# Low parts of the activations on VectorE, and two key chunks projected between the turns of the token tiles

## The chip, the cores and the metric

The kernel runs on one core of one Trainium2 chip, with its engines TensorE (PE), VectorE (DVE), ScalarE (ACT), GpSimd (POOL) and SyncE (SP). The metric is device time of one execution in microseconds, as the median of several runs.

## What is computed

One inference step of a one-layer hybrid decoder: 16 meta tokens and 1024 prompt tokens, with 8 single decode tokens beside them, 1048 tokens in all. Cut to the part that matters here:

```python
def rms_norm(x, g):
    xf = x.astype(jnp.float32)
    y = xf * lax.rsqrt(jnp.mean(xf * xf, axis=-1, keepdims=True) + EPS)
    return (y * g.astype(jnp.float32)).astype(x.dtype)
...
    n = rms_norm(x, g_mix)
    q, k, v, xr, gr, gates = jnp.split(n @ w_in, SPLITS, axis=-1)
...
    attn = attend(q, k, v, sb_bias.reshape(N_KV_HEADS, GROUP))
...
    x = x + (gate_a * attn + gate_b * rnn) @ w_out
...
    x = x + (jax.nn.gelu(ua) * ub) @ w_down
```

The first stage of the kernel makes n, turned so that the model dimension lies on the partitions, and from it k, v and q. All later stages (attention and the recurrent branch, output projection, FFN) are the same in both kernels.

## The kernel before

The stages are blocks that all five engines enter and leave together. The change lies in the first one, `phase_qkv`. Its inputs are 9 token tiles (tile 0 has 24 rows, tiles 1 to 8 have 128 each) and 12 weight tiles of 128 output columns: key tiles j = 0, 1, value tiles j = 2, 3, then 8 query tiles.

**Token tiles.** For tile t, in turn: SP loads it (`load_x`); ACT squares it with a running sum (`square`, L279); DVE makes the mean (L337), ACT its root (L292), DVE the reciprocal (L342) and the scaled rows in place (L343); PE turns it in 8 transposes into PSUM `xt` (L419); DVE multiplies by the gain into `tmp` (L356); ACT rounds `tmp` to the high part `n_hi` (L298); POOL takes tmp - n_hi as the low part `n_lo` (L260). `xt` and `tmp` have two halves that tiles use in turn. ACT and DVE run these loops with one tile's lag between the first steps and the last: in turn t, DVE does the mean, reciprocal and scaling of tile t and then the gain of tile t-1.

**Weights.** A weight tile is loaded into one of two slots of `w_raw`; ACT rounds it to `w_hi` (L285), POOL makes `w_lo` (L254).

**Projections.** `project` (L87) makes one chunk of 350 token columns: for each of 8 parts k of the model dimension three matmuls (high by high, weight high by activation low, weight low by activation high), 24 in all, summed in one of two PSUM banks `proj`. ACT takes it out (`evacuate`, L308) into `kv_ch` or `q_stage`. There are 3 chunks per weight tile; chunk 0 needs token tiles 0 to 3, chunk 1 tiles 0 to 6, chunk 2 all. Before the change PE starts them only when `lo_ready` shows all 9 tiles, and goes weight tile by weight tile. A slot's next `w_hi` is made by ACT behind the middle chunk of the following tile. After the four key and value tiles PE turns them back to token rows (L448), DVE copies these (L386) and SP stores them; then come the query tiles in a loop.

**Orders.** Every engine runs its list in the order written; semaphores (`lo_ready`, `w_lo_ready`, `proj_out` and others) tie them together. SP issues all transfers on one queue.

## Time and profile before

| | us |
|---|---|
| median of 3 runs | 2277.09 |
| lowest and highest | 2276.91, 2279.01 |
| the profiled execution | 2274.87 |
| its span in the trace | 2273.1 |

The profiled execution is 1.77 us longer than its span: that lies around the first and last instruction. All durations below are from this one execution. A row of the timeline gives the start, the duration, the engine and line, the instruction with output and inputs, how often it stands in a row, and in brackets how long its engine was idle before and what ended that.

### The profile page before, as it was taken

How to read it: one execution, taken by the hardware profiler on the slowest of the kernel's cores; microseconds unless marked ns; L12 is line 12 of the kernel's file. 1: busy time of each engine (PE TensorE's matmuls, PEld its weight loads, DVE VectorE, ACT ScalarE, POOL GpSimd, SP SyncE). 2: the span in 40 equal slices, each digit the busy share in tenths (PEclk: the TensorE clock that was granted, in tenths of full speed). 3: DMA queues.
4: the chain of work that ended last, by engine and by line, in shares of the span. 5: the costliest groups of instructions: out<-in, count | busy, mean ns of one | idle time of the engine just before them, and what ended most of it. 6: DMA issues, size and time to landing. Idle time of an engine off the chain costs nothing. (4 is left out here: it accounts for less than half of the span.)

```text
span 2273.1 us, 41388 instructions
## 1 busy us (share of the span) xinstructions
PE 1961.5 (86%) x14580; PEld 1773.7 (78%) x14580; DVE 1210.3 (53%) x2020; ACT 938.1 (41%) x1514; POOL 247.6 (11%) x117
## 2 busy tenths in 40 slices
PE   4997988879797978879798597899999999999985
PEld 3897867767685867758586386899999999999985
DVE  6101557556484756647474632655554555545555
ACT  4122567566656647666665411212221222212213
POOL 4121000000000000000000400312221222112210
PEclk9998999989899998989898798999999999999988
DMA  3233313131222212131221222111111111111104
GB/s 120 80 99 98 78 37 92 30 98 36 78 57 74 76 33 78 40 92 51 72 62 50 96 87 70 43 42 46 46 37 37 55 47 46 37 37 46 46 19 165
DMA packets 197465, 144.01 MB, mean 63 GB/s; under 512 B 58037, under 2 KB 186102, under 8 KB 197268
## 3 DMA queue, kind: packets, MB, share of 16 engines
q1 hardware_dynamic: 197294, 141.79, 21.7%
q8 instruction: 99, 1.62, 0.3%
q14 instruction: 72, 0.59, 0.1%
HBM read 124.38 MB, written 17.61 MB: 62 GB/s over the span
## 5 line engine op out<-in xcount | busy, mean ns | idle before, releaser
L87 PE MATMUL d_p_up<-n_hi,d_w_hi 128*128 128x350 f32 x1056 | 343.7, 325 | 14.0 <-POOL d_w_lo L1656 7.7
L87 PE MATMUL d_p_up<-n_lo,d_w_hi 128*128 128x350 f32 x1056 | 342.6, 324 | 0.0
L87 PE MATMUL d_p_up<-n_hi,d_w_lo 128*128 128x350 f32 x1056 | 342.4, 324 | 0.0
L87 PE MATMUL b_p_proj<-n_hi,b_w_hi 128*128 128x350 f32 x768 | 274.0, 357 | 53.6 <-ACT r_gr L990 32.6
L1803 DVE TENSOR_TENSOR mix<-mix,d_p_down 128x350 f32<-128x350 f32 x264 | 137.3, 520 | 325.1 <-PE d_p_down L1850 325.1
L1700 ACT ACTIVATE d_up<-d_p_up 128x350 f32<-128x350 f32 x132 | 60.6, 461 | 502.2 <-PE d_p_up L87 502.2
L87 PE MATMUL b_p_proj<-n_lo,b_w_hi 128*128 128x350 f32 x768 | 257.2, 335 | 0.0
L87 PE MATMUL b_p_proj<-n_hi,b_w_lo 128*128 128x350 f32 x768 | 256.6, 334 | 0.0
L941 ACT ACTIVATE b_sums<-b_p_z,b_bias 128x720 f32<-128x720 f32 (+16 forms) x136 | 94.8, 697 | 304.7 <-PE b_p_z L1222 256.4
L87 PEld LDWEIGHTS d_p_up<-n_hi,d_w_hi 128*128 128x128 f32 x1056 | 200.5, 190 | 15.0 <-POOL d_w_lo L1656 8.1
L87 PEld LDWEIGHTS b_p_proj<-n_hi,b_w_hi 128*128 128x128 f32 x768 | 154.7, 201 | 72.5 <-ACT r_gb L990 29.9
L87 PEld LDWEIGHTS d_p_up<-n_hi,d_w_lo 128*128 128x128 f32 x1056 | 200.5, 190 | 0.0
L87 PEld LDWEIGHTS d_p_up<-n_lo,d_w_hi 128*128 128x128 f32 x1056 | 200.4, 190 | 0.0
L1053 DVE TENSOR_TENSOR_SCAN b_sums<-b_sums 128x720 f32<-128x720 f32 (+16 forms) x136 | 171.1, 1258 | 21.5 <-ACT b_sums L977 16.2
L1850 PE MATMUL d_p_down<-d_a_hi,d_wd_hi 128*128 128x350 f32 x480 | 159.3, 332 | 23.8 <-DVE d_a_lo L1794 23.8
L1039 DVE COPY mix<-b_p_misc 128x64 f32 (+2 forms) x136 | 30.1, 221 | 271.8 <-PE b_p_misc L1253 264.1
L1656 POOL TENSOR_TENSOR d_w_lo<-w_raw,d_w_hi 128x1024 fp32r<-128x1024 f32 x45 | 114.2, 2548 | 519.7 <-ACT d_w_hi L1686 519.7
L1215 PE MATMUL b_p_z<-b_k_in,b_q_in 64*64 64x360 f32 (+16 forms) x1024 | 103.1, 464 | 76.8 <-issue 31.7
L1850 PE MATMUL d_p_down<-d_a_hi,d_wd_lo 128*128 128x350 f32 x480 | 158.2, 330 | 0.0
L1850 PE MATMUL d_p_down<-d_a_lo,d_wd_hi 128*128 128x350 f32 x480 | 157.7, 329 | 0.0
L87 PEld LDWEIGHTS b_p_proj<-n_lo,b_w_hi 128*128 128x128 f32 x768 | 153.5, 200 | 0.0
L87 PEld LDWEIGHTS b_p_proj<-n_hi,b_w_lo 128*128 128x128 f32 x768 | 152.6, 199 | 0.0
(248 smaller groups left out, 3921.7 us busy)
## 6 DMA issues: line engine op xcount, KB each, us to landing
w_raw<-in_w_in SPq DMA_DIRECT2D x45, 512.0 KB, 4.9
w_raw<-in_w_up SPq DMA_DIRECT2D x45, 512.0 KB, 3.9
b_page<-in_cache_k SPq DMA_DIRECT2D x128, 128.0 KB, 2.2
b_page<-in_cache_v SPq DMA_DIRECT2D x128, 128.0 KB, 2.1
w_raw<-in_w_down SPq DMA_DIRECT2D x22, 512.0 KB, 3.2
b_q_in<-q_scr SPq DMA_DIRECT2D x272, 32.0 KB, 2.2
q_scr<-a_q_stage SPq DMA_DIRECT2D x16, 260.0 KB, 3.4
mix<-in_x_prompt SPq DMA_DIRECT2D x8, 512.0 KB, 7.5
```

The lines of the kernel that those rows point to most:

```text
L87: last = pe.matmul(out, w[:, k, :], x[:, k, col:col + CW], start=(k == 0 and w is w_hi and x is x_hi), stop=(k == KT - 1 and w is w_lo))
L941: own.mark(act.activation(so, pz, ACT.Abs, bias=bias[:, 0:1]))
L1039: dve.tensor_copy(g.mix[:, bass.ds(i if s >= 0 else i - 1, 1), FIRST + q0:FIRST + q0 + nq] .rearrange("p a c -> p (a c)"), p_av[:, 0:nq]). ...
L1053: dve.tensor_tensor_scan(pos[:, ::-1], so[:, ::-1], pos[:, ::-1], 0.0, ALU.add, ALU.add)\
L1215: last = pe.matmul(banks[bank][QB * a:QB * (a + 1), 0:k1 - k0], q_in[rows, Q_AT[s], a, :], k_in[rows, k0:k1], start=True, stop=k1 <= diagonal)
L1656: pool.tensor_tensor(w_lo[:, slot, :, :], w_raw[:, raw, :, :], w_hi[:, slot, :, :].bitcast(F32), ALU.subtract).then_inc(lo_ready, 1)
L1700: act.activation(up[:, u % 2, CW * c:CW * (c + 1)], p_up[:, n % 2, 0:CW], ACT.Copy).then_inc(up_out, 1)
L1803: dve.tensor_tensor(to, to, p_down[:, n % 4, 0:CW], ALU.add).then_inc(down_out, 1)
L1850: last = pe.matmul(p_down[:, n % 4, 0:CW], w[:, k, P * tile:P * (tile + 1)], a[:, k, CW * c:CW * (c + 1)], start=(k == 0 and w is wd_hi an ...
```

## The change

1. **Low parts.** POOL's loop over the token tiles is gone. In turn t, DVE makes the low part of tile t-2 behind the gain of tile t-1; the mean of tile t+1 is taken a turn earlier. ACT squares two tiles ahead instead of one, so that the square of tile 1 stands ahead of the first root. Behind its turns 5 and 7 DVE also makes `w_lo` of the first two weight tiles; POOL keeps the other ten. ACT rounds these two weights in its turns 5 and 7 (before: 7 and 9).
2. **Order of chunks.** The first six chunks are those of both key tiles in pairs, `FIRST_PIECES` = (0,0), (1,0), (0,1), (1,1), (0,2), (1,2) as (tile j, chunk c). PE does the first half (12 matmuls) of piece 0 behind the transposes of token tile 5 and the second behind those of tile 6, and piece 1 likewise behind tiles 7 and 8; pieces 2 to 5 follow. From value tile j = 2 on the order is the old one. ACT takes piece 0 out behind its last `n_hi` and piece 1 just behind that.
3. **Transfers.** The first weight tile is loaded ahead of token tile 4 (before: behind it), the second ahead of tile 6 (before: behind tile 8). Each key tile's store waits for its last piece.

```diff
@@ -87,6 +87,9 @@
             last = pe.matmul(out, w[:, k, :], x[:, k, col:col + CW],
                              start=(k == 0 and w is w_hi and x is x_hi), stop=(k == KT - 1 and w is w_lo))
     return last
+
+
+FIRST_PIECES = [(j, c) for c in range(CHUNKS) for j in range(2)] + [(j, c) for j in (2, 3) for c in range(CHUNKS)]
 
 
 def phase_qkv(nc, g, sem):
@@ -171,9 +174,8 @@
                     sp.dma_start(rows[r:r + n, :], src).then_inc(rows_in, 16)
                 for t in range(2, TILES):
                     load_x(t)
-                    if t == 4:
-                        load_w(0, 1, K_COL)
-                load_w(1, 2, K_COL + P)
+                    if t in (3, 5):
+                        load_w(t // 2 - 1, t // 2, K_COL + P * (t // 2 - 1))
                 sp.dma_start(g.bias_all[:, :], g.sb_bias[0, :].partition_broadcast(P)).then_inc(bias_in, 16)
                 sp.dma_start(g.table[:, :],
                              g.page_table.rearrange("(o a) b -> o (a b)", o=1)).then_inc(bias_in, 16)
@@ -183,7 +185,7 @@
                 for n in (2, 3):
                     load_w(n % 2, n + 1, K_COL + P * n)
                 for j in range(2):
-                    sp.wait_ge(proj_out, 2 + CHUNKS * (j + 1))
+                    sp.wait_ge(proj_out, 2 + FIRST_PIECES.index((j, CHUNKS - 1)) + 1)
                     for h in range(2):
                         sp.dma_start(g.k_scr[2 * j + h, :, :],
                                      kv_ch[HD * h:HD * (h + 1), j, FIRST:LAST]).then_inc(k_stored, 16)
@@ -254,14 +256,6 @@
                     pool.tensor_tensor(w_lo[:, slot, :, :], w_raw[:, slot, :, :],
                                        w_hi[:, slot, :, :].bitcast(F32), ALU.subtract).then_inc(w_lo_ready, 1)
 
-                for t in range(TILES):
-                    c0, nr = token_tile(t)
-                    pool.wait_ge(hi_ready, t + 1)
-                    pool.tensor_tensor(g.n_lo[:, :, c0:c0 + nr], tmp[:, t % 2, :, 0:nr],
-                                       g.n_hi[:, :, c0:c0 + nr].bitcast(F32), ALU.subtract).then_inc(lo_ready, 1)
-                    if t == TILES - 2:
-                        low_part(0, 1)
-                low_part(1, 2)
                 with pool.Fori(0, 5, 1) as i:
                     for s in range(2):
                         low_part(s, nth(i, 2, s + 2))
@@ -284,35 +278,42 @@
                     act.wait_ge(proj_done, chunks)
                     act.activation(w_hi[:, slot, :, :], w_raw[:, slot, :, :], ACT.Copy).then_inc(w_hi_ready, 1)
 
+                def evacuate(bank, index, out, scale):
+                    act.wait_ge(proj_done, index + 6)
+                    act.activation(out, proj[:, bank, 0:CW], ACT.Copy, scale=scale).then_inc(proj_out, 1)
+
+                def kv_piece(p):
+                    j, c = FIRST_PIECES[p]
+                    evacuate(p % 2, p + 1, kv_ch[:, j, CW * c:CW * (c + 1)], 1.0)
+
                 square(0)
+                square(1)
                 for t in range(TILES + 1):
                     if t < TILES:
                         _, nr = token_tile(t)
                         act.wait_ge(meaned, t + 1)
                         act.activation(stat[0:nr, 2, t:t + 1], stat[0:nr, 1, t:t + 1], ACT.Sqrt).then_inc(rooted, 1)
-                    if t + 1 < TILES:
-                        square(t + 1)
+                    if t + 2 < TILES:
+                        square(t + 2)
                     if t:
                         c0, nr = token_tile(t - 1)
                         act.wait_ge(scaled, t)
                         act.activation(g.n_hi[:, :, c0:c0 + nr], tmp[:, (t - 1) % 2, :, 0:nr],
                                        ACT.Copy).then_inc(hi_ready, 1)
-                    if t in (7, 9):
-                        high_part((t - 7) // 2, 3 * (t - 5) // 2, 16)
+                    if t in (5, 7):
+                        high_part((t - 5) // 2, 3 * (t - 3) // 2, 16)
+                    if t == TILES:
+                        kv_piece(0)
                 act.activation(lam[:, 0, :], g.par[:, :, R_LAM], ACT.Abs).then_inc(act_step, 1)
+                kv_piece(1)
                 act.wait_ge(act_step, 1)
                 act.activation(lam[:, 1, :], lam[:, 0, :], ACT.Exp, scale=-1.0).then_inc(lam_exp, 1)
-
-                def evacuate(bank, index, out, scale):
-                    act.wait_ge(proj_done, index + 6)
-                    act.activation(out, proj[:, bank, 0:CW], ACT.Copy, scale=scale).then_inc(proj_out, 1)
-
-                for j in range(4):
-                    for c in range(CHUNKS):
-                        n = CHUNKS * j + c
-                        evacuate(n % 2, n + 1, kv_ch[:, j, CW * c:CW * (c + 1)], 1.0)
-                        if c == 1 and j:
-                            high_part((j + 1) % 2, 3 * (j + 2), 16 * ((j + 1) // 2 + 1))
+                for p in range(2, len(FIRST_PIECES)):
+                    kv_piece(p)
+                    if p in (4, 5):
+                        high_part(p - 4, 6 + p + 1, 32)
+                    if FIRST_PIECES[p] == (3, 1):
+                        high_part(0, 15, 48)
 
                 def q_pair(i, last):
                     for s in range(2):
@@ -330,12 +331,17 @@
             @block.vector
             def _(dve):
                 own = Chain(dve, dve_step)
-                for t in range(TILES + 1):
-                    if t < TILES:
-                        _, nr = token_tile(t)
-                        dve.wait_ge(squared, t + 1)
-                        dve.tensor_scalar(stat[0:nr, 1, t:t + 1], stat[0:nr, 0, t:t + 1], 1.0 / D, EPS,
-                                          ALU.mult, ALU.add).then_inc(meaned, 1)
+
+                def mean(t):
+                    _, nr = token_tile(t)
+                    dve.wait_ge(squared, t + 1)
+                    dve.tensor_scalar(stat[0:nr, 1, t:t + 1], stat[0:nr, 0, t:t + 1], 1.0 / D, EPS,
+                                      ALU.mult, ALU.add).then_inc(meaned, 1)
+
+                mean(0)
+                for t in range(TILES + 2):
+                    if t + 1 < TILES:
+                        mean(t + 1)
                     if t < TILES:
                         _, nr = token_tile(t)
                         dve.wait_ge(rooted, t + 1)
@@ -347,7 +353,7 @@
                         dve.tensor_copy(g.par[:, :, :].rearrange("p k r -> p (k r)"),
                                         pt[:, 0:KT * N_ROWS]).then_inc(params, 1)
                         dve.wait_ge(params, 1)
-                    if t:
+                    if 1 <= t <= TILES:
                         u = t - 1
                         c0, nr = token_tile(u)
                         dve.wait_ge(x_turned, u + 1)
@@ -356,6 +362,17 @@
                         dve.tensor_tensor(tmp[:, u % 2, :, 0:nr], xt[:, u % 2, :, 0:nr],
                                           g.par[:, :, R_GMIX:R_GMIX + 1].to_broadcast([P, KT, nr]),
                                           ALU.mult).then_inc(scaled, 1)
+                    if t >= 2:
+                        u = t - 2
+                        c0, nr = token_tile(u)
+                        dve.wait_ge(hi_ready, u + 1)
+                        dve.tensor_tensor(g.n_lo[:, :, c0:c0 + nr], tmp[:, u % 2, :, 0:nr],
+                                          g.n_hi[:, :, c0:c0 + nr].bitcast(F32), ALU.subtract).then_inc(lo_ready, 1)
+                    if t in (5, 7):
+                        n = (t - 5) // 2
+                        dve.wait_ge(w_hi_ready, n + 1)
+                        dve.tensor_tensor(w_lo[:, n, :, :], w_raw[:, n, :, :], w_hi[:, n, :, :].bitcast(F32),
+                                          ALU.subtract).then_inc(w_lo_ready, 1)
                 dve.wait_ge(bias_in, 32)
                 for h in range(2):
                     dve.tensor_copy(g.bias_pair[HD * h:HD * (h + 1), :], g.bias_all[HD * h:HD * (h + 1), h:HEADS:2])
@@ -410,6 +427,20 @@
             def _(pe):
                 pe.sem_inc(proj_done, 6)
                 pe.wait_ge(consts, 3)
+
+                def first_piece(p, k0, k1):
+                    j, c = FIRST_PIECES[p]
+                    if k0 == 0:
+                        pe.wait_ge(lo_ready, tiles_for_chunk(c))
+                        if c == CHUNKS - 1:
+                            pe.wait_ge(consts, 9)
+                        pe.wait_ge(w_lo_ready, j + 3)
+                        pe.wait_ge(proj_out, p + 1)
+                    last = project_part(pe, proj[:, p % 2, 0:CW], w_hi[:, j % 2], w_lo[:, j % 2],
+                                        g.n_hi, g.n_lo, CW * c, k0, k1)
+                    if k1 == KT:
+                        last.then_inc(proj_done, 1)
+
                 for t in range(TILES):
                     _, nr = token_tile(t)
                     pe.wait_ge(normed, t + 1)
@@ -425,8 +456,12 @@
                             last = pe.transpose(pt[:, N_ROWS * k:N_ROWS * (k + 1)], rows[:, P * k:P * (k + 1)],
                                                 g.ident[0:N_ROWS, 0:N_ROWS])
                         last.then_inc(rows_t, 1)
-                pe.wait_ge(lo_ready, TILES)
-                pe.wait_ge(consts, 9)
+                    if t in (5, 7):
+                        first_piece(t // 2 - 2, 0, KT // 2)
+                    if t in (6, 8):
+                        first_piece(t // 2 - 3, KT // 2, KT)
+                for p in range(2, 6):
+                    first_piece(p, 0, KT)
 
                 def tile(slot, index, first_chunk, base):
                     pe.wait_ge(w_lo_ready, index + 2)
@@ -437,7 +472,7 @@
                                        g.n_hi, g.n_lo, CW * c)
                         last.then_inc(proj_done, 1)
 
-                for n in range(4):
+                for n in (2, 3):
                     tile(n % 2, n + 1, CHUNKS * n, 0)
                 pe.wait_ge(proj_out, 2 + 12)
                 for t in range(TILES):
```

On VectorE, inside the token tiles of the first stage, before the change (a_stat holds the means and roots, mix the token rows, a_xt the turned tile in PSUM, a_tmp the tile times the gain):

```order
L337 TENSOR_SCALAR a_stat<-a_stat 128x1 [waits a_squared]
L342 RECIPROCAL a_stat<-a_stat 128x1 [waits a_rooted]
L343 TENSOR_SCALAR mix<-mix,a_stat 128x1024 [waits a_dve_step]
L356 TENSOR_TENSOR a_tmp<-a_xt,par 128x1024 [waits a_lo_ready,a_x_turned]
L337 TENSOR_SCALAR a_stat<-a_stat 128x1 [waits a_squared]
```

The same engine after the change, turn 5 and the start of turn 6:

```order
L348 RECIPROCAL a_stat<-a_stat 128x1 [waits a_rooted]
L349 TENSOR_SCALAR mix<-mix,a_stat 128x1024 [waits a_dve_step]
L362 TENSOR_TENSOR a_tmp<-a_xt,par 128x1024 [waits a_lo_ready,a_x_turned]
L369 TENSOR_TENSOR n_lo<-a_tmp,n_hi 128x8x128 [waits a_hi_ready]
L374 TENSOR_TENSOR a_w_lo<-w_raw,a_w_hi 128x1024 [waits a_w_hi_ready]
L338 TENSOR_SCALAR a_stat<-a_stat 128x1 [waits a_squared]
```

Each turn has one more operation over a whole tile, and turns 5 and 7 have two more.

On TensorE, the last token tile and the first projection before the change:

```order
L419 MATMUL a_xt<-ident,mix 128x128 [waits a_scaled,a_normed]
L419 MATMUL a_xt<-ident,mix 128x128 x7
L87 MATMUL a_proj<-n_hi,a_w_hi 128x350 [waits a_w_lo_ready,a_proj_out,a_consts,a_lo_ready]
L87 MATMUL a_proj<-n_lo,a_w_hi 128x350
L87 MATMUL a_proj<-n_hi,a_w_lo 128x350
```

After the change, the transposes of tile 5 and the first three of the 12 matmuls behind them:

```order
L450 MATMUL a_xt<-ident,mix 128x128 [waits a_scaled,a_normed]
L450 MATMUL a_xt<-ident,mix 128x128 x7
L87 MATMUL a_proj<-n_hi,a_w_hi 128x350 [waits a_proj_out,a_w_lo_ready,a_lo_ready]
L87 MATMUL a_proj<-n_lo,a_w_hi 128x350
L87 MATMUL a_proj<-n_hi,a_w_lo 128x350
```

The first projection has moved from behind tile 8 to behind tile 5, and the transposes of tiles 6 to 8 stand behind pieces of it.

On ScalarE, the start of the stage before the change:

```order
L279 ACT_TABLE_LOAD
L279 ACTIVATE a_junk,a_stat<-mix 24x1024 [waits a_x_in0]
L292 ACT_TABLE_LOAD
L292 ACTIVATE a_stat<-a_stat 24x1 [waits a_meaned]
L279 ACTIVATE a_junk,a_stat<-mix 128x1024 [waits a_x_in1]
```

And after it:

```order
L273 ACT_TABLE_LOAD
L273 ACTIVATE a_junk,a_stat<-mix 24x1024 [waits a_x_in0]
L273 ACTIVATE a_junk,a_stat<-mix 128x1024 [waits a_x_in1]
L295 ACT_TABLE_LOAD
L295 ACTIVATE a_stat<-a_stat 24x1 [waits a_meaned]
```

The square of tile 1, with its wait for that tile's transfer, now stands ahead of the table load and of the first root.

## Rows read from the trace of the kernel before

**Rows 1.** The page's first part: busy time, share of the span, instructions.

```profile
PE 1961.5 (86%) x14580; PEld 1773.7 (78%) x14580; DVE 1210.3 (53%) x2020; ACT 938.1 (41%) x1514; POOL 247.6 (11%) x117
```

**Rows 2.** Stretches: from:to, length, busy by engine, granted clock, DMA share, GB/s.

```profile
0.00:52.00 52.00, 18.80 (x84) 15.50 (x85) 35.10 (x42) 25.50 (x43) 23.26 (x25) 1.00 0.35 121
56.00:77.00 21.00, 20.88 (x131) 20.59 (x130) 0.22 (x2) 3.73 (x7) 2.39 (x1) 1.00 0.12 31
206.00:213.00 7.00, 0.00 (x0) 0.00 (x0) 1.14 (x7) 1.60 (x5) 1.56 (x6) 0.73 0.33 81
600.00:1200.00 600.00, 505.15 (x4764) 424.98 (x4764) 372.39 (x629) 382.39 (x632) 0.00 (x0) 0.91 0.25 64
```

**Rows 3.** Timeline of VectorE: tile 1's scaling, then a whole turn.

```profile
7.78 0.75 DVE L343 TENSOR_SCALAR mix<-mix,a_stat 128x1024 f32<-128x1024 f32 x1
...
21.74 1.21 DVE L356 TENSOR_TENSOR a_tmp<-a_xt,par 128x1024 f32<-128x1024 f32 x1
...
24.16 0.16 DVE L342 RECIPROCAL a_stat<-a_stat 128x1 f32<-128x1 f32 x1 [1.16 <-ACT a_stat L292]
24.36 2.49 DVE L343 TENSOR_SCALAR mix<-mix,a_stat 128x1024 f32<-128x1024 f32 x1
26.77 1.21 DVE L356 TENSOR_TENSOR a_tmp<-a_xt,par 128x1024 f32<-128x1024 f32 x1
27.90 0.14 DVE L337 TENSOR_SCALAR a_stat<-a_stat 128x1 f32<-128x1 f32 x1
```

**Rows 4.** Timeline of GpSimd in the same turn.

```profile
24.12 2.18 POOL L260 TENSOR_TENSOR n_lo<-a_tmp,n_hi 128x1024 fp32r<-128x1024 f32 x1 [2.85 <-ACT n_hi L298]
```

**Rows 5.** Timeline of ScalarE in the same turn.

```profile
22.98 1.06 ACT L298 ACTIVATE n_hi<-a_tmp 128x1024 fp32r<-128x1024 f32 x1 [2.84 <-DVE a_tmp L356]
23.95 0.18 ACT L292 ACTIVATE a_stat<-a_stat 128x1 f32<-128x1 f32 x1
24.04 1.04 ACT L279 ACTIVATE a_junk<-mix 128x1024 f32<-128x1024 f32 x1
```

**Rows 6.** Timeline of TensorE: tile 4, the first chunk's start and end of its ramp.

```profile
21.87 1.97 PE L419 MATMUL a_xt<-ident,mix 128*128 128x128 f32 x8 [3.06 <-DVE mix L343]
...
50.91 0.66 PE L87 MATMUL a_proj<-n_hi,a_w_hi 128*128 128x350 f32 x1 [6.94 <-POOL n_lo L260]
...
51.66 0.49 PE L87 MATMUL a_proj<-n_hi,a_w_lo 128*128 128x350 f32 x1
51.95 0.50 PE L87 MATMUL a_proj<-n_hi,a_w_hi 128*128 128x350 f32 x1
...
56.04 0.32 PE L87 MATMUL a_proj<-n_hi,a_w_hi 128*128 128x350 f32 x1
56.20 0.32 PE L87 MATMUL a_proj<-n_lo,a_w_hi 128*128 128x350 f32 x1
```

**Rows 7.** Timeline of ScalarE at the start: the second table load.

```profile
4.59 1.28 ACT L292 ACT_TABLE_LOAD   x1
```

**Rows 8.** Transfers issued in stretches of 5.0:5.4, 5.8:6.4 and 6.4:6.8, us to landing.

```profile
mix<-in_x_prompt SPq DMA_DIRECT2D x1, 512.0 KB, 3.8
mix<-in_x_prompt SPq DMA_DIRECT2D x2, 512.0 KB, 5.6
w_raw<-in_w_in SPq DMA_DIRECT2D x1, 512.0 KB, 7.7
```

**Rows 9.** Line 1019, a later stage: VectorE makes a weight's low part (ns min/median/max).

```profile
L1019 DVE TENSOR_TENSOR b_w_lo<-w_raw,b_w_hi x33: 1215/1224/1227, 213.5 to 1215.8; 128x1024 fp32r<-128x1024 f32 x33
```

**Rows 10.** Timelines of GpSimd and TensorE where the third weight tile begins.

```profile
74.12 2.39 POOL L254 TENSOR_TENSOR a_w_lo<-w_raw,a_w_hi 128x1024 fp32r<-128x1024 f32 x1 [20.93 <-ACT a_w_hi L285]
...
76.57 0.43 PE L87 MATMUL a_proj<-n_hi,a_w_hi 128*128 128x350 f32 x1
```

**Rows 11.** Timeline of TensorE: last key and value transposes, first query matmuls.

```profile
109.24 0.66 PE L448 MATMUL a_xt<-ident,a_kv_ch 128*128 128x128 f32 x4 [0.79 <-DVE a_kv_tok L386]
...
109.90 0.33 PE L87 MATMUL a_proj<-n_lo,a_w_hi 128*128 128x350 f32 x1
```

## The prediction

> **What bounds the kernel now.** The page's first part says PE is busy 86% of the span [rows 1], but that is a mean over stages. The stretches show what matters: in the first 52 us PE works 18.8 us, while from 56 to 77 us it is busy 20.88 of 21 [rows 2]. So the first stage has two parts: token tiles, bound by something else, and projections, bound by PE. In the first part the step from one tile to the next is 26.77 - 21.74 = 5.03 us [rows 3]. In that step VectorE's scaling of the rows takes 2.49 us, though the same instruction took 0.75 us on tile 1 [rows 3]. Beside the slow one GpSimd runs its low part from 24.12 to 26.30; the scaling begins at 24.36 and ends at 26.85, which is 0.55 after GpSimd is done [rows 3, 4]. I read this as the scaling waiting for GpSimd. ScalarE's own work per tile is about 2.2 us [rows 5] and the transposes are 1.97 [rows 6], so neither is the bound. PE then waits 6.94 us for the last low parts and starts projecting at 50.91 [rows 6]. The first six chunks last until 76.57, where the third weight tile begins [rows 6, 10]: 25.66 us. Matmuls come 0.29 apart at first (350 columns in 0.29 us is the 1.2 GHz level) and 0.16 apart from 55.7 on [rows 6]. The granted clock of the stretch says 1.00 there [rows 2]; I go by the pace, since the column seems blind until its first change. At full pace a chunk is 24 x 0.161 = 3.86 us, six are 23.2, so the ramp and small waits cost 25.66 - 23.2 = 2.5.
>
> **The tile step after the change.** VectorE alone: reciprocal to scaling 0.20, scaling 0.75 less 0.09 overlap (24.36 + 2.49 = 26.85 against the next start at 26.77) 0.66, gain 1.13 (26.77 to 27.90) [rows 3], new low part 1.14 (1.224 for a like 128x1024 subtraction [rows 9], less the same overlap), mean 0.07: 3.20 us. Its loop with ScalarE: gain 1.21, hand-over 0.04, n_hi 0.97 until the root starts, root 0.18, hand-over 0.04, then 0.20 and 0.66: 3.30 us [rows 3, 5]. The longer one decides, so a tile takes 3.3 us instead of 5.03. The low part's bounds are 1.05 and 1.3; both stay under or near the loop and move the end by 0.2 at most.
>
> **The start gets later.** The square of tile 1 now stands ahead of the table load of 1.28 us that was done by 5.9 [rows 7]. Tile 1's transfer lands near 5.5 (an estimate between the end of the load and 3.8 us after issue as for tile 2 [rows 8]); square with read-out 1.2, load 1.28, so the first root is at 8.0, against 5.9, and tile 0 is turned at 9.2. Running on by the same durations, tile 1 is turned at 11.3 and tile 2 at 13.7.
>
> **The transfers.** Tile 2 landed at 5.1 + 3.8 = 8.9, the first weight tile at 6.4 + 7.7 = 14.1, with tiles 3 and 4 between [rows 8], so about 1.7 us each. The weight now takes tile 4's place and tile 4 lands at about 14.1. ScalarE wants it at 12.5, behind the root of tile 2. It waits 1.6 us, n_hi of tile 1 is queued behind it and VectorE's low part and next root behind that: tile 3 is turned at 17.5. If tile 4 lands at 12.6 the end gains 0.5, if it lands at 15.6 the end loses 1.5. Later tiles land before they are wanted, by the same spacing. Then by 3.3: tile 4 at 20.8 (before: 21.87 [rows 6]), tile 5 at 24.1 (before: one step more, 26.9).
>
> **The pieces.** Behind tile 5 PE waits: n_hi of tile 4 from 25.2, rounding of the weight 26.2 to 27.2, its low part on VectorE 27.3 to 28.5. First half of piece 0 from 28.5: 12 x 0.293 = 3.5 us at the low pace, to 32.05. Transposes of tile 6 to 33.75 (here they delay the gain of tile 6: VectorE now waits for PE). Second half: PE has by then worked without a gap for over 5 us, and in the kernel before the pace rose 4.5 to 5 us into unbroken work [rows 6], so 12 x 0.161 = 1.9, to 35.7. Transposes of tile 7 at the full pace 1.3 (four take 0.66 [rows 11]), to 37.0. Piece 1 waits for the second weight: gain of tile 6 at 34.1, n_hi 35.3, rounding 36.3, low part 37.4 to 38.6. Half 38.6 to 40.6, tile 8 to 41.9, half to 43.8. Piece 2 needs the bank of piece 0, which ScalarE empties only behind the last n_hi: gain of tile 8 at 41.9, n_hi 43.1 to 44.1, out at 44.55. Here a wait of 0.8 us takes the place of the old one. So piece 2 starts at 44.6, four chunks of 3.86 take it to 60.05, and the third weight tile waits 0.2 us for its low part as before: in both orders the rounding stands behind the fifth chunk, and a copy-out of some 0.4 (an estimate: 350 of the 1024 columns that take 1.06 [rows 5]), the rounding of 1.05 [rows 5] and 2.39 on GpSimd [rows 10], with three hand-overs, just outlast the sixth chunk. It begins at 60.3 instead of 76.57.
>
> **Sum.** 76.57 - 60.3 = 16.3 us. Split another way: PE's main run begins 50.91 - 44.6 = 6.3 earlier, with two chunks (7.7) already done, and without the ramp and its small waits (2.3 of the 2.5). Behind the third weight tile nothing in the order has moved, and PE is the bound to the end of the stage, so this arrives at the end. The two key stores and the loads of the next weights come earlier than needed. The constants and bias copies on VectorE (small operations) lie beside the four chunks; if that cover were gone they would cost some 10 us, but PE does not wait for them before the value tiles are turned, 30 us later. In the profiled execution: span 2273.1 - 16.3 = 2256.8, with 1.8 around it 2258.6. The median lay 2.2 above the profiled execution, so 2260.8, **about 2261**.
>
> **One rule against the trace.** PE's clock must hold through the pieces. The trace shows that transposes alone, four per 1.45 us, with idle between, kept it high: the first query matmuls behind them run at the full pace (0.33 at 109.90) [rows 11], while in 7 us without work it fell to a mean of 0.73 [rows 2]. The Trainium skill, TensorE: Matmul & The Clock Gate, section Part 4: PE-mode transpose, says that transposes do not count as busy TensorE in the same way as matmuls. Taken strictly that would leave piece 0 and 1 at the low pace, which is rival B. The trace disagrees as to holding the clock; whether transposes help it to rise is shown nowhere.
>
> **Rivals.**
> B. *The clock stays low through both pieces.* The tile phase of the kernel before never left the low pace, with PE busy 1.97 of 5.03. Then the second half of piece 0 ends at 37.3, tile 7 at 39.0, piece 1 goes 39.0 to 42.5 and 44.2 to 47.7 with tile 8 between. PE never pauses, so piece 2 starts at 47.7. The four chunks pay the ramp once: 25.66 - 7.72 = 17.9, to 65.6. Saved 10.9: **2266.2**. For it: the gaps and the mixed work; against: no pause from 28.5 on.
> C. *The scaling is slow for another reason than GpSimd* (the change does not remove what it means to). With 2.49 kept, VectorE's step is 0.20 + 2.40 + 1.13 + 1.14 + 0.07 = 4.94 and the loop 5.04; tile 5 is turned at 32.8, the second weight and piece 1 come at 49.4, piece 2 at 57.0, the third weight tile at 72.7. Saved 3.9: **2273.2**, no change that counts. Against it: 0.75 whenever GpSimd is idle, and an end 0.55 behind GpSimd's.
> D. *More waits in the tile part than I count*: tile 4 at 16 or later and each turn of the loop 0.5 longer cost 2 + 6 x 0.5 = 5 us: about **2266 to 2270**.
> E. *Slower, by the clock of the later stages.* From 600 to 1200 us the granted clock is 0.91 [rows 2], so about 18% of the time is at the low level (0.5), and when it falls depends on how PE's pauses lie. The whole program moves 16 us, and the pauses may fall otherwise. Over the some 2000 us behind the first stage, with PE bound, a mean lower by 0.01 costs some 20 us. From a mean lower by 0.008 it eats the 16.3; lower by 0.011 it gives **2283**. Against it: the three runs lie within 2.1 us of each other.
>
> **How the numbers follow.** Chances: forecast A (2257 to 2264) 0.66, B 0.16, D 0.08, C 0.05, E 0.05. Predicted is A, 2261. The range: down, the clock already high in the first half of piece 0 (12 x 0.13 = 1.6 less) and tile 4 in time (0.5 less), with 2.4 for the median's own spread, gives 2256.5; up, B with half of the late tile (0.7) and 1.5 of spread gives 2268.5. It leaves out C, E and part of D, and holds some 0.85. A measurement of this kernel can tell about 0.2%, 4.6 us, from no change. Faster by more than that are A, B and D and a little of E, 0.91; within it C and little else, 0.05; slower 0.04.
>
> **What would show it.** The scaling at 0.75 us in every turn and a tile step of 3.2 to 3.5 us (C wrong). ScalarE idle before the square of tile 4. PE's first projection matmul near 28.5, 0.29 apart for about 12 of them and 0.16 in the second half of piece 0; in B all 48 are 0.29 apart. VectorE's gain of tile 6 released by PE. PE released by ScalarE's copy-out at about 44.6, and the third weight tile begun at 60.3. The time from there to the end as before, to 1 or 2 us; if it is longer by more, E is at work. I would be wrong if the low part on VectorE took over 1.7 us, or if ScalarE loaded its table more often than three times in the stage.

## The result, and the profile after

The changed kernel takes 2253.7 us (median of 4, 2248.4 to 2256.7) where the kernel before, timed beside it, takes 2277.0: a ratio of 0.9894, 95% interval 0.9874 to 0.9914. It is 23.3 us faster. The prediction was 2261.0 with a range of 2256.5 to 2268.5, so the direction is right and the saving is 7 us larger than forecast, outside the range. The profiled execution took 2253.84, with 1.8 of it outside the span.

The page's first part of the changed kernel (busy time, share, instructions):

```profile
span 2252.0 us, 41403 instructions
PE 1963.5 (87%) x14580; PEld 1776.4 (79%) x14580; DVE 1205.3 (54%) x2031; ACT 937.9 (42%) x1514; POOL 225.1 (10%) x106
```

As [rows 1], TensorE does the same 14580 matmuls in the same busy time. What went is idle time. The stretches that answer to [rows 2]:

```profile
0.00:52.00 52.00, 31.80 (x171) 29.37 (x172) 34.11 (x68) 26.79 (x46) 1.86 (x14) 0.84 0.38 132
56.00:77.00 21.00, 20.89 (x130) 20.60 (x129) 0.00 (x0) 4.64 (x8) 4.80 (x2) 1.00 0.39 102
...
600.00:1200.00 600.00, 517.03 (x4875) 434.41 (x4873) 376.55 (x642) 379.24 (x636) 0.00 (x0) 0.92 0.23 61
```

In the first 52 us TensorE is busy 31.80 instead of 18.80, which is what was meant. But the last row has moved too, and nothing had been changed there: from 600 to 1200 it is busy 517.03 instead of 505.15, with 4875 matmuls in place of 4764. A stage that the diff does not touch runs faster. That row is the first sign of where the other 7 us are.

Next to [rows 3], VectorE's timeline, a whole turn of the changed kernel:

```profile
20.36 1.22 DVE L362 TENSOR_TENSOR a_tmp<-a_xt,par 128x1024 f32<-128x1024 f32 x1
21.50 1.22 DVE L369 TENSOR_TENSOR n_lo<-a_tmp,n_hi 128x1024 fp32r<-128x1024 f32 x1
...
22.99 0.75 DVE L349 TENSOR_SCALAR mix<-mix,a_stat 128x1024 f32<-128x1024 f32 x1
23.66 1.22 DVE L362 TENSOR_TENSOR a_tmp<-a_xt,par 128x1024 f32<-128x1024 f32 x1
```

The scaling takes 0.75 us instead of 2.49, and the step is 23.66 - 20.36 = 3.30 instead of 5.03, though VectorE now makes the low part as well (1.22). TensorE's timeline with the pieces, next to [rows 6, 10]:

```profile
28.28 0.63 PE L87 MATMUL a_proj<-n_hi,a_w_hi 128*128 128x350 f32 x1 [2.50 <-issue]
...
31.91 1.15 PE L450 MATMUL a_xt<-ident,mix 128*128 128x128 f32 x8
...
34.82 1.03 PE L450 MATMUL a_xt<-ident,mix 128*128 128x128 f32 x8
...
37.72 0.40 PE L87 MATMUL a_proj<-n_hi,a_w_hi 128*128 128x350 f32 x1 [1.87 <-issue]
...
40.32 1.91 PE L450 MATMUL a_xt<-ident,mix 128*128 128x128 f32 x8
...
45.08 0.40 PE L87 MATMUL a_proj<-n_hi,a_w_hi 128*128 128x350 f32 x1 [0.80 <-ACT a_kv_ch L283]
...
60.86 0.43 PE L87 MATMUL a_proj<-n_hi,a_w_hi 128*128 128x350 f32 x1
```

Piece 0 begins at 28.28, piece 1 at 37.72, piece 2 at 45.08 behind ScalarE's copy-out, the third weight tile at 60.86 where [rows 10] had 76.57.

To see where the rest arose, the program is cut at marks that both traces have: the first projection matmul, the first score matmul of attention, the last one, and the end. Times in us, one profiled execution each:

| kernel | first projection | attention begins | attention lasts | from there to the end of the span |
|---|---|---|---|---|
| before | 50.9 | 218.9 | 1011.7 | 1042.5 |
| changed | 28.3 | 204.2 | 1002.7 | 1045.1 |

The first stage gave 14.7 us, attention 9.0, and the rest took 2.6 back. The forecast had 16.3, 0 and 0. The last of the three does not repeat: run again (below), both kernels take 1042.3 us from the last score matmul to the end.

### The profile page after: what moved, and what is told of

Its sections match the earlier page's. It is cut to its first block and busy times, and to the rows that moved or that the text cites. A ratio compares the mean times of both kernels' runs of the same rounds, so it can differ in the third digit from the quotient of the medians.

```text
span 2252.0 us, 41403 instructions
## 1 busy us (share of the span) xinstructions
PE 1963.5 (87%) x14580; PEld 1776.4 (79%) x14580; DVE 1205.3 (54%) x2031; ACT 937.9 (42%) x1514; POOL 225.1 (10%) x106
## 5 line engine op out<-in xcount | busy, mean ns | idle before, releaser
L1088 DVE TENSOR_TENSOR_SCAN b_sums<-b_sums 128x720 f32<-128x720 f32 (+16 forms) x136 | 171.1, 1258 | 20.5 <-ACT b_sums L1012 16.2
```

The lines of the kernel that those rows point to most:

```text
L1088: dve.tensor_tensor_scan(pos[:, ::-1], so[:, ::-1], pos[:, ::-1], 0.0, ALU.add, ALU.add)\
```

## Inside attention: the jump back

The attention loop is one loop of seven passes behind a first pass written out, so there are six jumps back. At the head of each pass TensorE stands idle before the first score product. The view of waits, of TensorE from 350 to 1212 before and to 1205 after (waited for: us in total, times, longest):

```profile
PE b_p_z L1215 <- issue: 31.7, 5, 7.4
...
PE b_p_z L1215 <- DMA b_k_in<-k_scr: 7.3, 1, 7.3
```

```profile
PE b_p_z L1250 <- DMA b_k_in<-k_scr: 19.1, 3, 6.7
...
PE b_p_z L1250 <- issue: 10.2, 3, 3.6
```

The first fence is the kernel before, the second the changed one. "issue" means that the engine waited for nothing that the profile shows. The kernel before has five such waits and one put down to a transfer of keys, 39.0 us in six passes. The changed one has three and three, 29.3 us. The difference, 9.7, is the 9.0 by which attention is shorter. Every second pass loads new keys; there the wait fell only from 6.3 to 7.4 us to 6.0 to 6.7, and it is the transfer that ends it now. In the other three it fell from 5.5 to 6.4 us to 3.3 to 3.6.

Something that the view of waits has no name for holds TensorE at the jump, and for a shorter time after the change. The page's list of DMA queues has a candidate, instructions themselves. The kernel before, then the changed one (packets, MB, share):

```profile
q8 instruction: 99, 1.62, 0.3%
```

```profile
q8 instruction: 93, 1.52, 0.3%
```

Six packets of 16384 bytes fewer, one for each jump. The pieces' extra waits make TensorE's program five instructions longer (8651 against 8646, of 64 bytes, counted in the built programs; the two traces too hold 2032 against 2027 records of TensorE ahead of attention, and all five more are waits), so every later instruction stands five places further on. In the kernel before the loop begins 216 instructions behind a multiple of 256, which is one packet, in the changed one 221. The Trainium skill, Runtime: NRT & Kernel Launch, section Instruction fetch mechanics, says that instructions arrive in blocks of 16 KiB, 256 of them, in sequence, and that a taken branch whose target is not among those at hand has to wait for the block to be fetched. The packets of 16384 bytes agree with it. It does not say that the target's place within its block matters; the runs below show that. The traces show one thing more: not every loop is fetched again. At the jumps of the first stage's query loop (298 instructions in the trace) and of the FFN's (908) the queue has no packet, and the next matmul comes 0.04 to 0.05 us behind the jump, in both kernels. Only the attention loop, with over 2180, brings packets in each pass. Where between 908 and 2180 the limit lies no run here shows.

## Experiments

Each is timed against the kernel before, run beside it. That kernel shows medians of 2280.0 (21 runs), 2278.8 (11), 2279.4 (15) and 2278.7 (19) in the four groups, from 2271.6 to 2285.4 in all, so the 2277 of the three runs that the prediction started from was itself on the low side, and its 2.1 us of spread told too little.

### The two kernels again

> The kernel before once more. Theory 1: its first stage ends at the same place (attention begins at 218.9 within 0.5 us), the attention stage takes other than 1011.5 us in this trace, by up to 9 us. Theory 2: 1011.5 us within 1 us, as the later stages would be fixed by the code.

Measured: 2282.1 us, ratio 1.0005 (0.9995 to 1.0014); attention 1018.9, 99 packets.

> The changed kernel once more, with its own trace. In the first trace of it the attention stage begins 14.7 us earlier than before, and the stages behind it are 6.4 us shorter as well (attention 9.0 shorter, FFN 2.7 longer), though no instruction in them differs. Theory 1 (the clock): where TensorE's clock falls in the attention and FFN stages depends on how the pauses lie when they begin, so the first stage is again 14 to 16 us shorter and the rest differs from trace to trace by several us in either direction; the times spread over some 8 us (2248 to 2257). Theory 2 (a lasting effect of the change on later stages): attention and FFN take again within 1 us what they took in the first trace (attention 1002.5 us from its first to its last score matmul).

Measured: 2257.3, ratio 0.9904 (0.9889 to 0.9919); attention 1004.8, 93 packets. So attention before (1011.7, 1018.9) and after (1002.7, 1004.8) do not overlap, though with 7.2 and 2.1 us between repeats neither theory held as written: the later stages are not fixed within 1 us, and yet the change has a lasting effect on them.

### One part at a time

Low parts on VectorE alone, with the squares and means moved ahead as in the change, and the old order of the projections (abridged: `[...]` stands for indices, and the lines that set them and those of ScalarE are left out):

```diff
-                for t in range(TILES):
-                    pool.wait_ge(hi_ready, t + 1)
-                    pool.tensor_tensor(g.n_lo[...], tmp[...], g.n_hi[...], ALU.subtract).then_inc(lo_ready, 1)
-                    if t == TILES - 2:
-                        low_part(0, 1)
+                low_part(0, 1)
...
+                    if t >= 2:
+                        u = t - 2
+                        dve.wait_ge(hi_ready, u + 1)
+                        dve.tensor_tensor(g.n_lo[...], tmp[...], g.n_hi[...], ALU.subtract).then_inc(lo_ready, 1)
```

> The kernel before with the low parts of the activations on VectorE and the squares two tiles ahead, but with the projections and transfers in their old order (GpSimd still makes all weight low parts). By my sum: a tile step of 3.3 us instead of 5.03, the first projection matmul at 38.5 to 40.5 instead of 50.9, the third weight tile at 64 to 66 instead of 76.6, attention 11 to 12.5 us earlier. Total about 2265.5. Rival (the scaling is not held up by GpSimd): step 5.0, attention at most 1 us earlier, total 2276.

Measured: 2274.6, ratio 0.9973 (0.9962 to 0.9984); first projection at 44.08. That is 4 to 6 us later than expected, the third weight tile (70.0) came as late, and the whole gained 5 us instead of some 12. The main reason is the best evidence in the study for the forecast's first step. VectorE, GpSimd and TensorE:

```profile
31.19 0.75 DVE L342 TENSOR_SCALAR mix<-mix,a_stat 128x1024 f32<-128x1024 f32 x1
...
35.44 2.65 DVE L342 TENSOR_SCALAR mix<-mix,a_stat 128x1024 f32<-128x1024 f32 x1
```

```profile
35.20 2.34 POOL L254 TENSOR_TENSOR a_w_lo<-w_raw,a_w_hi 128x1024 fp32r<-128x1024 f32 x1 [32.39 <-ACT a_w_hi L279]
```

```profile
38.14 1.97 PE L424 MATMUL a_xt<-ident,mix 128*128 128x128 f32 x8 [4.17 <-DVE mix L342]
44.08 0.66 PE L87 MATMUL a_proj<-n_hi,a_w_hi 128*128 128x350 f32 x1 [3.98 <-DVE n_lo L362]
```

The scaling takes 0.75 us in every turn but the last. In that one, the only turn in which GpSimd works (on a weight's low part), it takes 2.65 and ends 0.55 behind GpSimd's end. Same instruction, same kernel: the scaling is slow because GpSimd runs. Rival C falls. (This took 1.9 us; another 1.0 went to ScalarE's root behind the rounding of that weight, and the rest of the lateness was not followed up.) The attention loop shows the old picture: 1015.5 us, 99 packets.

The pieces alone, with the low parts of activations and of both weight tiles back on GpSimd (abridged; VectorE's lines for them are taken out):

```diff
+                for t in range(TILES):
+                    pool.wait_ge(hi_ready, t + 1)
+                    pool.tensor_tensor(g.n_lo[...], tmp[...], g.n_hi[...], ALU.subtract).then_inc(lo_ready, 1)
+                    if t in (4, 6):
+                        low_part((t - 4) // 2, (t - 2) // 2)
```

> The changed kernel with the low parts of activations and of the first two weights back on GpSimd, in the same turns. By my sum: tile step 5.0 us again, two chunks done between the tiles, the third weight tile at about 69 (67 to 71) instead of 76.6 before and 60.9 after; attention 6 to 9 us earlier than before. Total about 2269.5. If the two halves of the change are additive, low_only and this one together give more than the change's 14.7, since both use the same idle time of TensorE before 50.9.

Measured: 2262.3, ratio 0.9925 (0.9909 to 0.9942). The step of the tiles is the old 5.03, the first piece begins at 37.10, and attention begins at 216.0, 3 to 4 us earlier than before, where 6 to 9 were expected (the third weight tile at 72.8, not 67 to 71). The rest of its 17.7 us is attention: 1002.8 us and 93 packets. This kernel has TensorE's longer program and almost none of the first stage's gain; it separates the two for the first time.

### The place of the loop

The kernel before with five instructions more ahead of its projections, all of them waits on a count that is reached (two such waits make one instruction there):

```diff
                 pe.wait_ge(lo_ready, TILES)
                 pe.wait_ge(consts, 9)
+                for _ in range(10):
+                    pe.wait_ge(lo_ready, TILES)
```

> The kernel before with ten more waits on TensorE behind those for the last low part (on a count that has been reached by then, so they hold nothing up). They make TensorE's program five instructions longer ahead of the attention loop, as the changed kernel's is; nothing else differs, and the first stage does the same work in the same order. Placement theory (where the loop's first instruction stands in the 16384-byte packets in which instructions arrive decides how long the jump back to it waits): the instruction queue shows 93 packets as in the changed kernel instead of 99, the passes of the attention loop that don't wait for a transfer of keys begin after 3.3 to 3.6 us of idle TensorE instead of 5.5 to 6.4, attention takes 1003 to 1006 us instead of 1012 to 1019, and the whole is 6 to 10 us shorter than the kernel before: 2270 to 2274 against 2280. Rival, the clock (the shorter attention of the changed kernel comes of a granted clock that happens to fall later, or of what the first stage leaves behind): 99 packets, attention 1012 to 1019, time 2278 to 2282, no difference. Rival, the changed order itself (transfers of the second stage start earlier against the first stage): likewise no difference.

Measured: 2267.5, ratio 0.9945 (0.9932 to 0.9958); attention 1003.7, 93 packets. Five idle instructions make the kernel before 11.4 us faster (6 to 10 were expected), though its first projection came 2 us late (53.0), most of it from a token tile that was ready later.

The changed kernel with five instructions fewer:

```diff
-                        pe.wait_ge(lo_ready, tiles_for_chunk(c))
-                        if c == CHUNKS - 1:
+                        if j == 0:
+                            pe.wait_ge(lo_ready, tiles_for_chunk(c))
+                        if p == 4:
                             pe.wait_ge(consts, 9)
-                        pe.wait_ge(w_lo_ready, j + 3)
-                        pe.wait_ge(proj_out, p + 1)
+                        if p < 2:
+                            pe.wait_ge(w_lo_ready, j + 3)
+                        else:
+                            pe.wait_ge(proj_out, p + 1)
```

> The changed kernel without those waits of the first six pieces that an earlier wait has already covered (the low parts of the activations for a second tile of the same chunk, the weights for pieces 2 to 5, the copied-out banks for pieces 0 and 1, the constants for piece 5). TensorE's program is five instructions shorter, as long as that of the kernel before; the same work runs in the same order. Placement theory: 99 instruction packets, passes without a transfer of keys begin after 5.5 to 6.4 us of idle TensorE, attention takes 1012 to 1019 us, and the time is 2262 to 2266, 14 to 17 us below the kernel before (that is, what the first stage alone gives, as forecast) instead of 22 to 23. Rivals (clock, or the changed order): nothing changes, 2254 to 2258, attention 1002 to 1005.

Measured: 2265.3, ratio 0.9944 (0.993 to 0.9958); attention 1018.8, 99 packets. The first stage is as quick as in the changed kernel (attention begins at 203.3), and the extra gain is gone: the kernel takes 8 to 13 us more than the changed one. Heads of one and the same pass, without new keys, in TensorE's timeline: the kernel before (run again), before with five more, changed with five fewer, changed.

```profile
858.55 1.48 PE L1215 MATMUL b_p_z<-b_k_in,b_q_in 64*64 64x360 f32 x8 [6.04 <-issue]
```

```profile
854.03 1.08 PE L1217 MATMUL b_p_z<-b_k_in,b_q_in 64*64 64x360 f32 x8 [3.57 <-issue]
```

```profile
840.83 1.48 PE L1253 MATMUL b_p_z<-b_k_in,b_q_in 64*64 64x360 f32 x8 [7.02 <-issue]
```

```profile
833.67 0.95 PE L1250 MATMUL b_p_z<-b_k_in,b_q_in 64*64 64x360 f32 x8 [3.27 <-issue]
```

The wait follows the position in both kernels and nothing else. The clock and the changed order as causes fall. The clock adds a little on top: behind the long waits it stands at its lower level (granted 0.50 from 858.5 to 860.0 in the first of the four) and the eight products take 1.48 us; with five more it is 0.71 from 854.0 to 855.2, in the changed kernel 0.83 from 833.6 to 834.6, and they take 1.08 and 0.95.

### The first stage by itself

Both kernels cut off behind their first stage; attention, the FFN and the outputs they write are left out:

```diff
+        return
         g.wo_arr = [sem(f"wo_arr{s}") for s in range(2)]
```

> The kernel before cut off behind its first stage (projections of keys, values and queries); attention, the feed-forward stage and the outputs that they write are left out. Without the attention loop this and its partner measure the first stage alone. Expected span 213 to 222 us, the last projection matmul at 205 to 207. It is the base for the next run.

> The changed kernel cut off in the same way: attention, the feed-forward stage and their outputs are left out. If the forecast's mechanism (third weight tile begins at 60.3 instead of 76.57) is the whole gain of the first stage and the rest of the 22 to 23 us arises behind it, this is 14 to 16 us shorter than the cut-off kernel before. If the first stage gives more than its own trace rows show (its end or its hand-over to attention is faster too), the difference is 18 us or more.

Measured: 214.15 (212.46 to 215.84) and 197.65 (196.32 to 198.24), 4 runs each. The difference is 16.5 us. That lies between the two cases told apart beforehand (14 to 16, or 18 and more), much nearer the first. The forecast's 16.3 for this stage was right; the runs of the two kernels spread over 3.4 and 1.9 us, so an agreement to 0.2 is partly luck.

### How the place acts

The same kernel with 69, 149, 2 and 240 instructions more than before. Of these the two are made like the five above, the others like this (for 69; the 240 are 125 here and 115 ahead of the attention loop):

```diff
-                pe.wait_ge(consts, 3)
+                for _ in range(1 + 2 * 69):
+                    pe.wait_ge(consts, 3)
```

> The kernel before with 69 more instructions on TensorE (138 repeated waits on a count that is reached) at its program's start instead of five. The attention loop is 2185 instructions, that is 8 packets of 256 and 137 over. The run with five more showed that the loop's start then stands 0 to 4 instructions behind a packet's start, and in the kernel before 1 to 5 ahead of it. With 69 more it stands 64 to 68 behind it, so the loop still touches 9 packets. Placement theory: as with five more, 93 packets (94 with the longer program), attention 1002 to 1006 us, 2266 to 2272. Rival (the gain hangs on the loop's first instruction being the first of a packet, or on the extra waits having been where they were): the gain is gone, attention 1012 or more, 2277 to 2282. The added instructions run while TensorE waits for the first token tile and should cost at most 2 us.

> The same with 149 more. The attention loop's start now stands 144 to 148 instructions behind a packet's start: the loop touches 10 packets again, as in the kernel before, but at the jump back it has over 100 instructions left in its first packet, where the kernel before has 1 to 5. Theory A (what costs is the jump to the last few instructions of a packet, since a second packet has to arrive before TensorE has work): the passes without a transfer of keys begin after 3.3 to 3.6 us idle, attention 1002 to 1006. Theory B (what costs is the tenth packet, wherever the start stands): 5.5 us and more of idle at the head, attention 1012 or more. Either way the queue shows 99 packets or more, since the loops of the first and of the feed-forward stage gain a packet too. Time by A 2266 to 2274, by B 2277 to 2284.

> The kernel before with two more instructions on TensorE (four repeated waits) ahead of its main projections. Five more gave 93 packets and the short waits, none gave 99 and the long ones. If the cost hangs on one sharp position, this run shows one of the two pictures whole: either 93 packets, heads of 2.9 to 3.8 us and attention of 1002 to 1006 us, or 99, 5.5 to 7.6 and 1012 to 1019, and it narrows the position to two or three instructions. A picture between them (heads of 4 to 5 us, attention 1007 to 1011) would speak against a position and for a cost that grows with the number of instructions left in the packet.

> The kernel before with 240 more instructions on TensorE, 125 at the program's start and 115 ahead of the attention loop, where TensorE waits for keys anyway. The loop's start stands 17 to 21 instructions ahead of a packet's start, where the kernel before has 1 to 5 and the run with 149 more some 110. Theory of the second packet: after the jump 17 to 21 instructions run (the first score products, 1 to 2 us), then TensorE stalls for the packet behind them; heads of 3 to 4 us with a new wait of 1 to 3 us inside the first score products, attention 1008 to 1016, and five or six packets more than the 94 or 95 of a program of that length. Rival (only the last five instructions ahead of a packet's start matter): attention 998 to 1006 and no such wait. The whole time is lengthened by what the 125 instructions hold up the first transposes, some 8 us, so the attention loop decides and not the time.

Measured, with the runs above; "left" is the number of instructions from the loop's first to the end of its packet, if a packet begins 219 to 221 behind the multiple of 256 (see below):

| more than before | left | packets | wait at heads without new keys | attention | time, ratio |
|---|---|---|---|---|---|
| 0 | 3 to 5 | 99 | 5.5 to 6.6 | 1011.7, 1018.9 | 2282.1, 1.0005 (0.9995 to 1.0014) |
| 2 | 1 to 3 | 99 | 6.3 to 6.5 | 1016.5 | 2279.1, 1.0004 (0.9992 to 1.0015) |
| 5 | 254 to 256 | 93 | 2.9 to 3.6 | 1003.7 | 2267.5, 0.9945 (0.9932 to 0.9958) |
| 69 | 190 to 192 | 94 | 3.2 to 3.7 | 1003.6 | 2266.3, 0.9936 (0.9920 to 0.9951) |
| 149 | 110 to 112 | 94 | 3.1 to 3.4 | 998.6 | 2276.8, 0.9987 (0.9978 to 0.9997) |
| 240 | 19 to 21 | 100 | 3.1 to 3.6, then 1.4 to 2.1 more | 1001.6 | 2283.5, 1.0028 (1.0013 to 1.0042) |

Two more change nothing, five more change all, so the packet's border lies 219 to 221 behind the multiple. Why it does not lie on the multiple itself is not shown; 35 to 37 instructions ahead of the program would do it. With 149 more the attention loop is as short as any, so it is not the number of packets that the loop touches (theory A of that expectation, not B); the time is long because the added waits hold up the first transposes (first projection at 61.7, where the kernel before has 50.9 and 51.2; I had allowed 2 us, it was 10 to 11). Its packets, 94, are not the 99 that I expected: I had counted packets for the loops of the first stage and the FFN, which bring none. From one jump to the next this kernel has 10 packets, as the changed one does, where the kernel before has 11.

The run with 240 shows the mechanism open. Its TensorE timeline at the head of a pass:

```profile
858.33 1.48 PE L1217 MATMUL b_p_z<-b_k_in,b_q_in 64*64 64x360 f32 x8 [3.33 <-issue]
861.50 0.26 PE L1224 MATMUL b_p_z<-b_never,b_ident_b 64*64 64x64 bf16 x2 [1.70 <-issue]
```

After the jump 3.33 us pass, eight score products run (16 instructions with their weight loads, and a few waits and register steps), then TensorE stops for another 1.70 us. In the other kernels the next products follow at once, as in the one with 149 more:

```profile
857.61 0.84 PE L1216 MATMUL b_p_z<-b_k_in,b_q_in 64*64 64x360 f32 x8 [3.30 <-issue]
858.28 0.20 PE L1223 MATMUL b_p_z<-b_never,b_ident_b 64*64 64x64 bf16 x2
```

The trace has each packet of the instruction queue with its own time, and that shows the cause itself. One jump without new keys of each kind, in us behind the jump (a packet from its start to its end):

| kernel | first packet | second packet | first product | ninth product |
|---|---|---|---|---|
| before (jump at 585.55) | 1.0 to 2.2 | 4.3 to 5.4 | 6.7 | 8.0 |
| changed (829.84) | 1.0 to 1.9 | 4.1 to 5.1 | 3.8 | 4.6 |
| 149 more (853.34) | 1.4 to 2.4 | 5.2 to 6.2 | 4.3 | 4.9 |
| 240 more (854.44) | 1.0 to 2.0 | 4.8 to 5.8 | 3.9 | 7.1 |

Two packets come behind every jump, one after the other. With the loop's start in its old place the first product waits for the second packet: in all 15 such jumps of the five traces with 5 or fewer left it comes 1.3 to 1.6 us behind that packet's end. In the 27 of the nine other traces it comes before the second packet has ended, 1.8 to 2.1 us behind the end of the first. With 240 more the ninth product again comes 1.3 to 1.6 us behind the end of the second.

So the jump waits some 3.3 us for the packet with its target, and the packet behind it comes some 3 us later (the ninth product stands 2.8 to 3.2 us behind the first). A target with 110 or more instructions left covers that; one with 20 left runs them and stops; one with 5 or fewer shows both waits as one of 5.5 to 7.0 us. In passes with new keys the second wait lies under the wait for keys, and there is next to no such stop (the ninth product comes 1.3 to 1.4 us behind the first). The 1001.6 us of attention are low only because its first pass begins later, with 20.7 us of waiting ahead of it, and is 8 us shorter; passes 2 to 8 take 895 us, against 888 with five more, and 898 and 904 in the two traces of the kernel before. The rival (only the last five places matter) fails.

### A better version

Four moves in the changed kernel's first stage, each against a wait seen in its trace (abridged: the lines that these replace further down are left out, and `weight_low` is VectorE's subtraction for one weight tile, as before):

```diff
-                    if t in (3, 5):
-                        load_w(t // 2 - 1, t // 2, K_COL + P * (t // 2 - 1))
+                    if t in (4, 6):
+                        load_w(t // 2 - 2, t // 2 - 1, K_COL + P * (t // 2 - 2))
...
+                    if t in (5, 7):
+                        high_part((t - 5) // 2, 3 * (t - 3) // 2, 16)
+                    if t == TILES - 1:
+                        kv_piece(0)
                     if t:
                         c0, nr = token_tile(t - 1)
                         act.wait_ge(scaled, t)
...
+                    if t == 7:
+                        weight_low(1)
                     if 1 <= t <= TILES:
```

> The changed kernel with four moves in its first stage and nothing else: the two weight loads stand behind token tiles 4 and 6 instead of 3 and 5; the high part of each is made ahead of the turn's n_hi on ScalarE, in time that it waits; the low part of the second is made on VectorE in turn 7 ahead of the multiply instead of at the turn's end; and the first piece is copied out in turn 8 instead of behind the last n_hi. Expected by the changed kernel's trace: the wait of 1.33 us for token tile 4 goes, the 0.94 us that VectorE waits for each high part, the 1.87 us ahead of the second piece, and the 0.80 us ahead of the third piece. The third piece begins at 41 to 43 instead of 45.1, the third weight tile at 57 to 59.5 instead of 60.9, and the whole is 2 to 4 us shorter than the changed kernel: 2250 to 2253 where that one has 2253 to 2257. If TensorE's clock falls for longer because the pieces then follow closer on the transposes, the gain is under 1 us. TensorE's program is as long as in the changed kernel, so the attention loop should stay at 1002 to 1005 us.

> The changed kernel once more, beside the kernel with the four moves on the same chip. Expected 2253 to 2258, attention 1002 to 1005, third weight tile at 60.6 to 60.9.

Measured: 2247.6 (ratio 0.9856, 0.9838 to 0.9874) beside 2252.1 (0.9891, 0.9871 to 0.9910), so 4.5 us by the medians; the two intervals still touch. TensorE's timeline of the better version:

```profile
27.07 0.63 PE L87 MATMUL a_proj<-n_hi,a_w_hi 128*128 128x350 f32 x1 [1.48 <-issue]
...
30.70 1.39 PE L454 MATMUL a_xt<-ident,mix 128*128 128x128 f32 x8
...
33.86 1.04 PE L454 MATMUL a_xt<-ident,mix 128*128 128x128 f32 x8
...
36.64 1.04 PE L454 MATMUL a_xt<-ident,mix 128*128 128x128 f32 x8
...
55.18 0.43 PE L87 MATMUL a_proj<-n_hi,a_w_hi 128*128 128x350 f32 x1
```

From 27.07 on TensorE has no wait up to the third weight tile, which begins at 55.18 against 60.25 in the changed kernel beside it. Attention begins at 197.8 against 203.6. That is more than the 2 to 4 us that I expected, because the waits ahead of pieces 1 and 2 and the low pace between them went together. The pieces leave no wait of TensorE there, so the next gain has to come from the time ahead of 27.07.

## Why the prediction was right, and where it failed

**GpSimd slows the scaling.** Right. 0.75 in every turn and a step of 3.30, as worked out; the partial kernel shows cause and effect within one trace.

**The start, and the transfer of tile 4.** Right: ScalarE's square of tile 4 waited 1.33 us for its transfer (1.6 forecast), tile 3 was turned at 17.2 (17.5), tile 4 at 20.5 (20.8), tile 5 at 23.8 (24.1).

**The pieces.** Right within a microsecond: 28.28 (28.5), 37.72 (38.6), 45.08 (44.6), third weight tile 60.86 (60.3). The two errors of the last two have a cause: piece 1 began 0.9 earlier, and then the pace fell to 0.29 apart from 38.91 to 42.3, which made the transposes of tile 8 take 1.91 us instead of the 1.3 counted. In the changed kernel run beside the better one this drop did not come, and the third weight tile began at 60.25.

**The clock rule.** Rival B fell: the second half of piece 0 ran at 0.16 apart. In the changed kernel the pace rose during the transposes of tile 6, which took 1.15 us for eight, where low pace gives 1.97 and full pace 1.03 (the forecast counted 1.3); ahead of them stood twelve matmuls without a gap. Whether transposes help the pace to rise, which the forecast called shown nowhere, the same trace shows further up:

```profile
13.69 1.74 PE L450 MATMUL a_xt<-ident,mix 128*128 128x128 f32 x8 [0.32 <-DVE mix L349]
17.21 1.09 PE L450 MATMUL a_xt<-ident,mix 128*128 128x128 f32 x8 [1.77 <-DVE mix L349]
20.50 1.97 PE L450 MATMUL a_xt<-ident,mix 128*128 128x128 f32 x8 [2.21 <-DVE mix L349]
```

Up to there TensorE had done nothing but transposes, and those of tile 3 took 1.09 us; the granted clock is 0.87 from 17 to 19 us and 0.50 from 19 to 20. It need not rise there: in the changed kernel run again the transposes of tile 3 took 1.97. For holding the clock, where the forecast leant against the rule, it was too bold: behind the last key and value transposes the query matmuls began at the low pace, 0.29 apart from 93.63 to 96.4, where [rows 11] had the full one. The stretch of 90 to 100 us, before and changed (columns as in [rows 2]):

```profile
90.00:100.00 10.00, 10.00 (x64) 10.00 (x63) 0.00 (x0) 1.87 (x3) 2.00 (x1) 1.00 0.17 48
```

```profile
90.00:100.00 10.00, 8.07 (x42) 7.60 (x43) 2.77 (x4) 0.46 (x1) 0.00 (x0) 0.83 0.81 267
```

The granted clock is 0.83 of 2.4 GHz as a mean of this stretch, after some 9 us in which TensorE did nothing but transposes with waits between. That agrees with the Trainium skill, TensorE: Matmul & The Clock Gate, section Part 4: PE-mode transpose, by which transposes do not count as busy in the same way as matmuls, and which the forecast had set aside on the strength of one place where the pace had held; the rise at tile 3 does not agree with it. It cost about 1.3 us (ten matmuls, 0.13 each) and accounts for the difference between 76.57 - 60.86 = 15.7 and the 14.7 us that reached attention. But the fall is not the change's doing. The kernel before, run again, has it too: its first twelve steps of query matmuls take 3.36 us, against 2.00 in [rows 11]'s trace and 3.52 in the changed kernel's. Of all 16 traces only that one and the one with the low parts alone kept the clock there. So the forecast had leant on the odd trace, and pairs in which both kernels fall gave more: 15.9 in the pair run again (219.9 against 204.0), 16.5 for the stage cut off. The forecast was 16.3.

**The step that failed** is this one: "Behind the third weight tile nothing in the order has moved, and PE is the bound to the end of the stage, so this arrives at the end." The order had not moved, but the instructions had, by five places, and that took 7 to 17 us out of attention (1002 to 1005 against 1012 to 1019). The idle time ahead of the first products of the six passes is 39 to 43 us with the loop in its old place and 28 to 30 in its new one. I had asked of the extra waits in each piece only what they wait for (nothing), not what they do by being there. The trace of before had the sign: five waits of 5.5 to 7.4 us at the loop's head, with no releaser, which I had not looked into since nothing there was to change. Rival E did allow for the later stages, but only by the clock and only as a loss. That nothing else failed is shown by the changed kernel with five instructions fewer: it does the same work in the same order with the loop back in its old place, and its 2265.3 us lie inside the forecast's range.

**The range** failed for the same reason: its lower end took in 1.6 + 0.5 of better first stage and 2.4 of spread. The base was a little low as well, since over 66 further runs the kernel before has medians of 2278.7 to 2280.0. With the base at 2279.5, the first stage's 16.3 and attention's 9 in the profiled pair one gets 2254.2, and the changed kernel's three medians are 2253.7, 2257.3 and 2252.1.

## What to carry to other kernels

When an edit changes how many instructions an engine's program holds, even by waits that wait for nothing, look at those later loops of that engine that are fetched again in each pass: the wait at the head, with no releaser, in the kernel before, and the packets of the instruction queue. Here that was the loop of 2185 instructions; those of 298 and 908 brought neither a packet nor a stop. Where such a head shows about 6 us and a few idle instructions ahead of the loop bring it to about 3, the loop's start stood just ahead of a packet's border, and a comparison of two versions of anything earlier in the program is off by that until both have the same picture. And test a stage's forecast by the stage alone: cut off, this one gave 16.5 us for a forecast of 16.3, while the whole was off by 7.
